# Two transformer blocks on one core: late sines in the latent front, 64-row rope halves with a signal per tile, and norms whose last tile goes in two halves

## What is computed

```python
def modulate(t, g, shift, scale):
    return rmsnorm(t, g) * (1.0 + scale[:, None, :]) + shift[:, None, :]

proj = h @ w_in                       # 1024 -> 384 + 256 + 64
cq, ckv, k_rope = jnp.split(proj, [384, 384 + 256], axis=-1)
q  = (rmsnorm(cq, g_q) @ w_q_up).reshape(B, S, 8, 128 + 64)
kv = (rmsnorm(ckv, g_kv) @ w_kv_up).reshape(B, S, 8, 128 + 128)
q_rope = apply_rope(q_rope, cos, sin) # t1*cos - t2*sin, t1*sin + t2*cos
k_rope = apply_rope(k_rope, cos, sin)
s = (q_nope . k_nope + q_rope . k_rope) * scale   # causal softmax, 8 heads
x = x + g1 * (softmax(s) @ v @ w_out)
```

## Time and profile before

| what | before |
| --- | --- |
| median of three runs | 3111.9 us |
| the profiled execution | 3115.64 us |
| its span | 3113.8 us |
| TensorE busy | 98% |
| VectorE, ScalarE, POOL busy | 52%, 37%, 57% |
| mean granted TensorE clock | 0.995 |

### The profile page before, as it was taken

How to read it: one execution, slowest core, us unless ns; L and a number is a source line. 1 busy time by engine, 2 the same in 40 slices (tenths; PEclk the granted TensorE clock), 3 DMA queues, 4 the chain that set the end, 5 groups by cost and what they waited for, 6 DMA issues and landing times.

```text
span 3113.8 us, 43914 instructions
## 1 busy us (share of the span) xinstructions
PE 3052.3 (98%) x14616; PEld 2486.9 (80%) x14616; DVE 1604.6 (52%) x2800; ACT 1143.7 (37%) x1479; POOL 1761.4 (57%) x2020
## 2 busy tenths in 40 slices
PE   7999999999999999999999999999999999999998
PEld 5887888876778887887788888888888888888887
DVE  7857555234445542995239995444401544444443
ACT  4554222246432223333333335555543323233322
POOL 2535776644267764975446754444445766666663
PEclk9999999999999999999999999999999999999999
DMA  8315555422145542222224445555564665555652
GB/s 323 107 35 209 199 192 172 132 74 75 46 147 197 190 161 90 98 88 80 95 91 142 144 136 196 179 179 194 199 218 144 210 211 200 194 174 187 216 192 77
DMA packets 170202, 481.95 MB, mean 155 GB/s; under 512 B 15360, under 2 KB 48896, under 8 KB 168080
## 3 DMA queue, kind: packets, MB, share of 16 engines
q1 hardware_dynamic: 147680, 410.83, 39.9%
q10 hardware_dynamic: 22448, 70.14, 5.7%
HBM read 411.70 MB, written 69.21 MB: 154 GB/s over the span
## 4 chain that ended last, share of the span: by engine, by line
PE 58%; POOL 21%; issue 18%; DVE 2%; ACT 1%; DMA 1%; POOLq 0%; SPq 0%; ACTq 0%; DVEq 0%
PE ps L1797 53%; POOL w_lo L563 21%; PE pa L1797 4%; DVE ada L1123 0%; DMA e_g<-expert_act 0%; DMA cols<-in_cols 0%; DVE s_tmp L1642 0%; DVE mg_lo L1644 0%; DVE h_lo L1193 0%; DVE sq L1187 0%; ACT mg_hi L972 0%; DVE s_m L1640 0%; DVE x L1176 0%; POOLq L561 0%; ACT w_hi L584 0%
## 5 line engine op out<-in xcount | busy, mean ns | idle before, releaser
L563 POOL TENSOR_TENSOR w_lo<-raw,w_hi 128x256 fp32r<-128x256 f32 x2016 | 1761.2, 906 | 1323.0 <-ACT w_hi L584 1321.9
L1797 PE MATMUL ps<-h_hi,w_hi 128*128 128x512 f32 x2392 | 945.0, 395 | 17.5 <-ACT h_hi L656 9.0
L1797 PE MATMUL ps<-h_hi,w_lo 128*128 128x512 f32 x2392 | 935.2, 391 | 0.0
L1797 PE MATMUL ps<-h_lo,w_hi 128*128 128x512 f32 x2392 | 911.7, 390 | 0.0
L584 ACT ACTIVATE w_hi<-raw 128x1024 fp32r<-128x1024 f32 x509 | 539.5, 1061 | 818.4 <-PE ps L1797 689.8
L1797 PEld LDWEIGHTS ps<-h_hi,w_hi 128*128 128x128 f32 x2392 | 451.3, 189 | 118.2 <-issue 12.8
L1797 PEld LDWEIGHTS ps<-h_hi,w_lo 128*128 128x128 f32 x2392 | 451.2, 189 | 95.6 <-issue 0.2
L1797 PEld LDWEIGHTS ps<-h_lo,w_hi 128*128 128x128 f32 x2392 | 450.6, 188 | 92.5 <-issue 0.7
L1797 PE MATMUL ps<-wa_hi,w_hi 128*128 128x512 f32 x1024 | 398.5, 389 | 0.4 <-DVE x L1761 0.4
L1797 PE MATMUL ps<-wa_hi,w_lo 128*128 128x512 f32 x1024 | 398.4, 389 | 0.0
L1797 PE MATMUL ps<-wa_lo,w_hi 128*128 128x512 f32 x1024 | 398.3, 389 | 0.0
(11 more groups left out here) (329 smaller groups left out, 3064.8 us busy)
## 6 DMA issues: line engine op xcount, KB each, us to landing
ada<-in_ada SPq DMA_DIRECT2D x144, 512.0 KB, 4.3
raw<-in_expert_u SPq DMA_DIRECT2D x128, 512.0 KB, 4.1
raw<-in_expert_v SPq DMA_DIRECT2D x128, 512.0 KB, 4.2
raw<-in_ffn_in SPq DMA_DIRECT2D x88, 512.0 KB, 3.5
expert_act<-g_act ACTq DMA_DIRECT2D x128, 256.0 KB, 4.2
gate_matrix<-w_st ACTq DMA_DIRECT2D x16, 2048.0 KB, 6.8
e_w<-gate_matrix SPq DMA_DIRECT2D x16, 2048.0 KB, 11.4
e_g<-expert_act SPq DMA_DIRECT2D x128, 256.0 KB, 7.6
```

Of the source, the lines that this page charges most:

```text
L563: last = nc.gpsimd.tensor_tensor(w_lo[:, k, c:c + 256], raw[:, k, c:c + 256], w_hi[:, k, c:c + 256].bitcast(F32), ALU.subtract)
L1797: return nc.tensor.matmul(out, a, b, start=start, stop=stop_)
```

## The change

Four things. First, in `act_mla` the wait for the angles and the two sine activations move from ahead of `latent(0)` to behind the last `latent_hi`, and `dve_mla` no longer waits for them ahead of the latents' scaling; `m_pos` and `m_ang` move from 82K and 84K to 16K and 18K of the arena (the place of `m_qr`), as `c_lo` takes 82K earlier now. Second, the weights of the rope parts are laid out so that the halves to be swapped are 64 rows, two heads interleaved; ScalarE swaps with two copies. The key rope is added once over all rows and multiplied with a 0/1 column per head parity. Third, in the up-projections each tile raises a signal: the last of a block `blk_done` as before, the others `up_mm`. Fourth, norms 1, 2, 3, 6 and 7 pass their last tile in halves of 256 tokens (TA, TB) through add, square, ones-product (two banks), Ln and Exp, and norms 1, 2, 3 and 6 also their first tile through scale and shift; the load of the table set stands ahead of the last square, and `KEEP_BUSY` is 2.

```diff
-KEEP_BUSY = 3
+KEEP_BUSY = 2
...
+    HALVED = {1: 0, 2: 1, 3: 2, 6: 3, 7: 4}
+    TA, TB = slice(0, S // 2), slice(S // 2, S)
...
+            if k == DT - 1 and n in HALVED:
+                nc.scalar.preload_act_table_set(LN_EXP)
+                act.wait_ge(xa_done, HALVED[n] + 1)
+                nc.scalar.activation(nsq[:, 3, TA], x[:, k, TA], ACT.Square).then_inc(sqa_ready, 1)
+                act.wait_ge(tile_free, X_TILE[n] + k + 1)
+                nc.scalar.activation(nsq[:, 3, TB], x[:, k, TB], ACT.Square).then_inc(sq_ready, 1)
+                break
...
+        act.wait_ge(ssa_done, u + 1)
+        nc.scalar.activation(rstd[:, TA], pa[:, 0, TA], ACT.Ln, scale=1.0 / D, bias=EPS).then_inc(lnh_done, 1)
         act.wait_ge(ss_done, NTH[n])
-        own_a.link(act, nc.scalar.activation(rstd[:, :], pa[:, 0, :], ACT.Ln, scale=1.0 / D, bias=EPS))
-        nc.scalar.activation(rstd[:, :], rstd[:, :], ACT.Exp, scale=-0.5).then_inc(rs_ready, 1)
+        nc.scalar.activation(rstd[:, TB], pa[:, 2, TB], ACT.Ln, scale=1.0 / D, bias=EPS).then_inc(lnh_done, 1)
+        act.wait_ge(lnh_done, 2 * u + 1)
+        nc.scalar.activation(rstd[:, TA], rstd[:, TA], ACT.Exp, scale=-0.5).then_inc(rsa_ready, 1)
+        act.wait_ge(lnh_done, 2 * u + 2)
+        nc.scalar.activation(rstd[:, TB], rstd[:, TB], ACT.Exp, scale=-0.5).then_inc(rs_ready, 1)
...
+        if k == 0 and n in HALVED:
+            act.wait_ge(ta_ready, HALVED[n] + 1)
+            nc.scalar.activation(h_hi[:, k, TA], NORM_BUF[n][:, k, TA], ACT.Identity, bias=shift)
+            act.wait_ge(t_ready, DT * H_USE[n] + 1)
+            nc.scalar.activation(h_hi[:, k, TB], NORM_BUF[n][:, k, TB], ACT.Identity, bias=shift).then_inc(hh_ready, 1)
+            return
...
+    def up_signal(last, t):
+
+        last.then_inc(blk_done if up_last(t) else up_mm, 1)
...
-        act.wait_ge(ang_done, 1)
-        nc.scalar.activation(m_sin[:, :], m_ang[:, :], ACT.Sin, scale=const("sign", 1))
-        nc.scalar.activation(m_cos[:, :], m_t[:, :], ACT.Sin).then_inc(trig_done, 1)
         for t in range(4):
             latent(t)
...
-        for q in range(4):
-            nc.scalar.activation(m_sw[32 * q:32 * q + 32, :], krope[32 * (q ^ 1):32 * (q ^ 1) + 32, :], ACT.Copy)\
-              .then_inc(k_raw, 1)
+        for q in range(2):
+            nc.scalar.activation(m_sw[64 * q:64 * q + 64, :], krope[64 * (1 - q):64 * (2 - q), :], ACT.Copy).then_inc(k_raw, 1)
...
         for t in range(3, 5):
             latent_hi(t)
+        act.wait_ge(ang_done, 1)
+        nc.scalar.activation(m_sin[:, :], m_ang[:, :], ACT.Sin, scale=const("sign", 1))
+        nc.scalar.activation(m_cos[:, :], m_t[:, :], ACT.Sin).then_inc(trig_done, 1)
         T = T0["mla_qn"]
         for t in range(12):
-            m = M0["mla_q"] + t // 2
-            hi.upto(m + 3)
-            act.wait_ge(blk_done, m + 1)
+            hi.upto(M0["mla_q"] + t // 2 + 3)
+            up_wait(act, t)
...
+    def dve_add(bank, gate, k, norm):
+
+        if k == DT - 1 and norm in HALVED:
+            nc.vector.scalar_tensor_tensor(out=x[:, k, TA], in0=bank[:, TA], scalar=gate, in1=x[:, k, TA],
+                                           op0=ALU.mult, op1=ALU.add).then_inc(xa_done, 1)
+            nc.vector.scalar_tensor_tensor(out=x[:, k, TB], in0=bank[:, TB], scalar=gate, in1=x[:, k, TB],
+                                           op0=ALU.mult, op1=ALU.add).then_inc(tile_free, 1)
+            return
...
-        dve.wait_ge(trig_done, 1)
         for a, tiles in enumerate((range(0, 3), range(3, 5))):
...
+        step(v.tensor_tensor(m_t[:, :], m_t[:, :], m_sw[:, :], ALU.add))
         for a in range(2):
-            mine, other = slice(ROPE * a, ROPE * (a + 1)), slice(ROPE * (1 - a), ROPE * (2 - a))
-            v.memset(m_kr[a][other, :], 0.0).then_inc(kr_done, 1)
-            v.tensor_tensor(m_kr[a][mine, :], m_t[mine, :], m_sw[mine, :], ALU.add).then_inc(kr_done, 1)
+            v.tensor_scalar(m_kr[a][:, :], m_t[:, :], consts[:, CONST["head"] + a:CONST["head"] + a + 1], None, ALU.mult)\
+              .then_inc(kr_done, 1)
...
+        if n in HALVED:
+            mm(pa[:, 0, TA], ones, rstd[:, TA], True, False)
+            mm(pa[:, 2, TB], ones, rstd[:, TB], True, False)
+            pe.wait_ge(sqa_ready, HALVED[n] + 1)
+            mm(pa[:, 0, TA], ones, nsq[:, 3, TA], False, True).then_inc(ssa_done, 1)
+            pe.wait_ge(sq_ready, DT * (NTH[n] + 1))
+            mm(pa[:, 2, TB], ones, nsq[:, 3, TB], False, True).then_inc(ss_done, 1)
```

More of the change, by code:

```diff
@@ L108 @@
 ))
-CONST = starts((("ident", 128), ("ones", 128), ("iota", 128), ("causal_t", 128), ("freq", 1), ("sign", 1),
+CONST = starts((("ident", 128), ("ones", 128), ("iota", 128), ("causal_t", 128), ("freq", 1), ("sign", 1), ("head", 2),
                 ("invcnt", 4 * PPAD)))
@@ L126, in make_consts @@
     put("freq", (THETA ** (-np.arange(0, ROPE, 2) / ROPE)).astype(np.float32)[p % (ROPE // 2)][:, None])
-    put("sign", np.where(p % ROPE < ROPE // 2, -1.0, 1.0)[:, None])
+    put("sign", np.where(p < ROPE, -1.0, 1.0)[:, None])
+    put("head", np.stack([p // (ROPE // 2) % 2 == a for a in range(2)], axis=1).astype(np.float32))
     t = np.arange(PPAD)
@@ L821, in act_ffn, with up_last, up_wait @@
         hi.skip(2 * FT)
+    def up_last(t):
+        return t % 2 == 1 if t < 12 else t % 4 == 3
+    def up_wait(eng, t):
+        if up_last(t):
+            eng.wait_ge(blk_done, M0["mla_q"] + (t // 2 + 1 if t < 12 else 6 + (t - 12) // 4 + 1))
+        else:
+            eng.wait_ge(up_mm, sum(not up_last(u) for u in range(t + 1)))
+    def up_signal(last, t):
+        last.then_inc(blk_done if up_last(t) else up_mm, 1)
     def act_mla(act, hi):
@@ L874, in act_mla @@
                 j = t - MH
-                act.wait_ge(kr_done, 6)
+                act.wait_ge(kr_done, 4)
                 if j >= 2:
@@ L878, in act_mla @@
                 dst = (m_sw, m_kraw)[j % 2]
[L879 to L880 removed]
+                for q in range(2):
+                    nc.scalar.activation(dst[64 * q:64 * q + 64, :], bank[64 * (1 - q):64 * (2 - q), :], ACT.Copy)\
                       .then_inc(sw_done, 1)
@@ L1179, in dve_norm @@
         dve.wait_ge(mod_done, MOD_STAGE[n])
-        for k in range(DT):
+        gain = modg[:, MODG[n]:MODG[n] + 1]
+        dve.wait_ge(rsa_ready, HALVED[n] + 1)
+        nc.vector.scalar_tensor_tensor(out=NORM_BUF[n][:, 0, TA], in0=x[:, 0, TA], scalar=gain, in1=rstd[:, TA],
+                                       op0=ALU.mult, op1=ALU.mult).then_inc(ta_ready, 1)
+        dve.wait_ge(rs_ready, NTH[n] + 1)
+        nc.vector.scalar_tensor_tensor(out=NORM_BUF[n][:, 0, TB], in0=x[:, 0, TB], scalar=gain, in1=rstd[:, TB],
+                                       op0=ALU.mult, op1=ALU.mult).then_inc(t_ready, 1)
+        for k in range(1, DT):
             dve_scale(n, k)
@@ L1183, in dve_norm @@
             dve_lo(dve, n, k)
+    def dve_add(bank, gate, k, norm):
[5 more added lines that the diff above has]
+            return
+        nc.vector.scalar_tensor_tensor(out=x[:, k, :], in0=bank, scalar=gate, in1=x[:, k, :],
+                                       op0=ALU.mult, op1=ALU.add).then_inc(tile_free, 1)
     def dve_scale(n, k, r=rstd):
@@ L1205, in dve_residual @@
             dve.wait_ge(blk_done, m + blocks * (k + 1))
-            nc.vector.scalar_tensor_tensor(out=x[:, k, :], in0=ps[:, (T + k) % RING, :],
-                                           scalar=mod[:, GATE[n] + k:GATE[n] + k + 1], in1=x[:, k, :],
-                                           op0=ALU.mult, op1=ALU.add).then_inc(tile_free, 1)
+            dve_add(ps[:, (T + k) % RING, :], mod[:, GATE[n] + k:GATE[n] + k + 1], k, norm)
     def dve_gla(dve):
@@ L1760, in add @@
                 dve.wait_ge(tile_free, T + DT * (g - 1) + k + 1 if i is None else i * (2 * DT) + (T + DT * (g - 1) + k + 1))
-            v.scalar_tensor_tensor(out=x[:, k, :], in0=ps[:, (T + k) % RING, :], scalar=mod[:, GATE[6] + k:GATE[6] + k + 1],
-                                   in1=x[:, k, :], op0=ALU.mult, op1=ALU.add).then_inc(tile_free, 1)
+            dve_add(ps[:, (T + k) % RING, :], mod[:, GATE[6] + k:GATE[6] + k + 1], k, norm)
         for k in range(GE):
@@ L1776, in dve_peer @@
             dve_squares(dve, 7, k - 1)
-            add(NG - 1, k)
+            add(NG - 1, k, None, 7)
     def dve_program(dve):
@@ L1823, in pe_norm @@
         pe.wait_ge(acc_done, 6 * NTH[n])
+        if n in HALVED:
[5 more added lines that the diff above has]
+            mm(pa[:, 2, TB], ones, nsq[:, 3, TB], False, True).then_inc(ss_done, 1)
+            if n < 7:
+                for _ in range(KEEP_BUSY):
+                    mm(pa[:, 3, :], ones, consts[:, 0:S], True, True)
+            return
         mm(pa[:, 0, :], ones, rstd[:, :], True, False)
```

56 lines of the change are left out of this document (28 added, 28 removed).

## The result

The changed kernel takes 3095.47 us in the median of four runs (3089.64 to 3096.74), the kernel before 3111.53 us beside it (3108.25 to 3112.51). The ratio is 0.9945, with a 95% interval of 0.9933 to 0.9957. The forecast was 3092.1 us, range 3086 to 3104: faster, as said, 3.4 us less than said. The profiled execution went from 3115.64 to 3095.24 us, its span from 3113.8 to 3093.4, 20.4 us less.

The account below looks back on a forecast made before the run. TensorE was taken as the bound, busy 3052.3 us, 98% of the 3113.8 us span. The terms, 8.18+7.2-1.2+5.6=19.8 us off the median of 3111.9 us, gave 3092.1 us, range 3086 to 3104.

Parts of the forecast that it names:

- Latent front: Latent front: TensorE's 5.38 us wait for w_lo and the slow tile behind it would go, 8.18 us saved.
- Up-projections: Up-projections: a signal per tile and 64-row halves would remove all pauses and restarts, 7.2 us of 53.39 us.
- the lower bound: Up-projections: if only the 64-row halves help, the saving is 4.4 us.
- Late sines: Before the first query eviction: moved sines make TensorE wait at the fifth query tile, 1.2 us lost with restart.
- about keep up: Rope tiles: VectorE's three steps of 0.69 us would nearly match TensorE's pace, with four banks between.
- Rival (a): Up-projections: first eviction 1.1 us later still, restarted tile cold for 2.6 us; 3.7 us more, 3095.8 us, chance 0.13.
- The further 1.4 us: Sine-table load: by the skill page, a drain besides the load would put the time 1.4 us above the forecast.
- Norm chains: Five norm boundaries: last tiles in halves and an earlier table load would save 5.6 us, bounds 0 and 8.0.
- Fillers: Norm boundaries: KEEP_BUSY 3 to 2 would cost 0, at most 2.6 us; 2.7 us idle at two-norm boundary, clock 1.00.
- Rival (d): Five boundaries: less filler drops the clock to 1.2 GHz; at two tiles of 24 matmuls, 48 us, 3140, chance 0.07.
- three signs of being wrong: Whole kernel: a cold stretch behind a boundary, a second wait in the up-projections, a span above 3104.
- Term 2: Up-projections: a signal per tile and 64-row halves remove 7.2 us of pauses; 4.4 us if only the halves help.

Follow-up runs that it names:

- the kernel with fillers: Changed kernel with sec_in block 3's copy ahead of the plain norm's Ln and four filler products, not two, at the two-norm boundary: 3096.67 us, 0.9958.
- the early copy: Changed kernel with the weight copy of sec_in block 3 issued ahead of the plain norm's Ln and Exp; alone 3093.71 us, 0.9951.

## Why the prediction was right, and where it was off

**Latent front.** Right in mechanism and size, 8.17 against 8.18 us. Undoing it brings back 5.57 us of wait and the half clock behind.

**Up-projections.** 7.2 us were forecast for signals and halves. Without the sines' cost the stretch goes from 53.39 to 46.57 or 46.28 us, 6.8 to 7.1. The three places (quarter copies, block signals, restarts) are the ones named. Their shares were not as reckoned: the lower bound gave the halves 4.4 us and the signals 2.8; undone one by one, beside the late sines, the signals give 4.0 and the query's halves 1.3.

**Late sines.** The term that was mis-sized: 1.2 us forecast, 2.0 to 2.3 measured. The wait at the fifth query tile came as worked out: 0.98 us, with restart 1.37-0.23=1.14. The rest, some 1.0 us, lies at the rope tiles, where the forecast had VectorE "about keep up": the wait of 0.27 us and slow restarts. ScalarE is not late there: ahead of the first rope tile's copies it stands 0.49 us for TensorE (its line at 710.29 above). Behind it one VectorE step took four times its 0.69 us, while POOL was splitting blocks (timelines of VectorE and POOL in the changed kernel):

```profile
712.21 2.66 DVE L1577 TENSOR_TENSOR m_sw<-m_sw,m_sin 128x512 f32<-128x512 f32 x1
```

```profile
710.79 3.53 POOL L570 TENSOR_TENSOR w_lo<-raw,w_hi 128x256 fp32r<-128x256 f32 x5
```

With early sines the same step took 1.68 us and TensorE lost 0.2 us at the rope tiles, with the sines behind the fourth tile 0.84 us and nothing. That this step is why TensorE waited there, and why it was slow just then, is argued from these rows, not shown by a run of its own. Rival (a), a cold restart behind the sines, did not happen: the clock of the stretch is 1.00. The further 1.4 us that followed from the Trainium skill's page ScalarE: Activation LUTs, section What ACT_TABLE_LOAD costs, did not come either: ScalarE's copies end at 695.66, the load starts at 695.68 and ends at 696.96, and the sine starts at 696.97, so the trace leaves no room for the page's drain.

**Norm chains.** 4.93 us instead of 5.6. Two links of 256 columns were taken too low: the shift takes 0.51 and 0.49 us instead of 0.41, and Ln of the second half starts 0.43 us behind that of the first instead of 0.31, as its sum ends at 650.85. Ahead of FFN 0 the square waited 0.6 us for the table load instead of 0.5. Adds, Exp and scale came as reckoned.

**Fillers.** The step that failed in kind: idle of 2.7 us at the two-norm boundary was to leave the clock at 1.00. The idle is 2.64 us, and the clock behind it 0.66. It cost nothing in the end, since a warm TensorE waits there for POOL; the forecast had not seen that cover. Rival (d) was thus right about one boundary of five and wrong in its length: some eight matmuls, not 48.

**Its own signs.** Of the three signs of being wrong that the prediction listed, two came: a cold stretch behind a boundary, and a second wait in the up-projections (0.27 us for `m_qr`). The time stayed right because the first was covered and the second small. The upper end of the range also left out Term 2's own lower bound, 2.8 us more; it was not needed.

**The total.** The terms measure 17.9 instead of 19.8 us. The remaining 1.5 us of the 3.4 between forecast and median are within the spread of the runs. That the two profiles differ by 20.4 is not a better forecast: FFN waits of 4.07 us that were in one execution and not in the other fill the gap.

## What to carry to other kernels

On an engine that runs in order, ask of each wait what stands behind it for somebody else: here eleven idle microseconds of ScalarE cost TensorE eight, because a weight copy stood behind the angles. When such work is moved, put it where the ring of banks is drained and not where it fills; behind four evictions the sines cost nothing, ahead of the first they cost two. Compare two traces stage by stage before crediting a change with the whole difference, since waits on DMA arrival, and cold stretches that no edit touches, come and go from trace to trace.

## What was not expected of the hardware

**The clock after a short idle is not settled by the idle alone.** Six traces have 2.64 us of idle at the two-norm boundary: in five, the changed kernel's among them, the granted clock in the 5 us behind was 0.66 or 0.67, in the kernel with block signals 1.00. After 2.41 us the router's transposes took 2.79 us in one execution and 1.50 in another. After 1.78 and 0.93 us it stayed at 1.00. What decides between is open. The stretch of the kernel with block signals:

```profile
1225.70:1230.70 5.00, 4.97 (x22) 4.17 (x23) 5.00 (x9) 4.97 (x9) 0.00 (x0) 1.00 0.01 3
```

**POOL hardly moves beside a run of VectorE's steps with two tensors in memory.** In the changed kernel as well the first split behind the boundary lasts 4.73 us and ends 0.6 us after VectorE's run; the next one, with VectorE idle, takes 0.74 (VectorE's and POOL's timelines):

```profile
1228.46 5.39 DVE L1205 SCALAR_TENSOR_TENSOR x<-x,cols,rstd 128x512 f32<-128x512 f32 x8
```

```profile
1229.72 4.73 POOL L570 TENSOR_TENSOR w_lo<-raw,w_hi 128x256 fp32r<-128x256 f32 x1 [18.75 <-ACT w_hi L591]
...
1234.41 0.74 POOL L570 TENSOR_TENSOR w_lo<-raw,w_hi 128x256 fp32r<-128x256 f32 x1
```

Measured from the end of VectorE's run, the kernel with fillers starts its split 4.7 us earlier, and it lasts 4.7 us longer: none of the time bought by the early copy was of use. The Trainium skill, page GPSIMD Engine Reference, section Key points, says that POOL shares its memory interfaces with VectorE and contends with VectorE's instructions that have two inputs in SBUF, the on-chip memory. These rows agree, and give a size. To leave a gap in VectorE's run for POOL was not tried.
